# Recurrent heads of a hybrid decoder step: maxima spread by one float32r product, sample outputs in four 32-row groups, prompt states of two heads at once

## The chip, the cores and the metric

The kernel runs on one core of one Trainium2 chip. The metric is the device time of one launch in microseconds (us); less is better. Five engines work side by side: TensorE (PE in the profile; PEld is its weight load), VectorE (DVE), ScalarE (ACT), GpSimd (POOL) and SyncE (SP), which issues most of the transfers.

## The reference, cut to what matters

One inference step of a two-layer trunk over 256 prompt tokens and 8 sample sequences of 8 tokens (320 token columns in all), with a model width of 1024. Layer 0 is half-FFN, mLSTM matrix memory with 8 heads (key width 64, value width 128), half-FFN. Layer 1 is half-FFN, block-sparse attention, half-FFN. The change touches the mLSTM heads alone. For each head, with b the running sum of the log forget gates, li the log input gates, c and n the carried state:

```python
d = jnp.where(causal, b[..., :, None] - b[..., None, :] + li[..., None, :], -jnp.inf)
m_loc = jnp.maximum(b + m, max(d));  w_intra = exp(d - m_loc);  w_inter = exp(b + m - m_loc)
sw = einsum('bhtd,bhsd->bhts', qc, kc) * w_intra
num = w_inter * einsum('bhtd,bhde->bhte', qc, c) + einsum('bhts,bhse->bhte', sw, vc)
den = maximum(abs(w_inter * einsum('bhtd,bhd->bht', qc, n) + sum(sw)), exp(-m_loc));  hc = num / den
c_new = a * c + einsum('bhs,bhsd,bhse->bhde', w, kc, vc)
```

The prompt starts from a zero state, each of the 8 sample sequences from a state of its own. Then hc is normalised per head, multiplied by a sigmoid gate and projected by w_out_a.

## The kernel before, in words

All large products are made in three float32r passes: `passes` (lines 405 to 407) multiplies a high and a low part of the weights with a high and a low part of the activations, 320 columns wide. A chunk is 128 output features over eight 128-row steps, so 24 passes. Weights come by the SP queue into four buffers; ACT (line 844) and DVE (line 1162) split each into `w_hi` and `w_lo`. Every other product is plain float32, which shows in the trace as two passes (two weight loads and two matmuls) for each call; a transpose is one pass.

The stage of the heads runs from the first `head_outputs` to the last. The order on PE is written out by hand. For each head h: `head_outputs(h)`, `head_scores(h + 1)`, `o_chunk(h + 1)` (24 passes of the output-gate projection, which give the other engines time), `head_turn(h)`.

- `head_scores(h)`: line 572 spreads row h of `neg` (minus the running maxima, and the inter-chunk weights, 384 columns) over 128 partitions with an 8-row selector; lines 573 to 575 make the scores of the prompt and the samples from `kT` and `qT`, 64 rows deep.
- DVE `decay(h)` (lines 1368 and 1374) adds columns and masks into `dmat` and makes `qm`, the sample queries spread by sequence; ACT (line 969) takes the exponential; DVE `weights(h)` (line 1383) multiplies scores and weights into `pmat` and raises `p_done`.
- `head_outputs(h)` waits for `p_done`: lines 592 to 594 the prompt outputs, line 596 (64 rows) the samples' own tokens, line 598 four products of `qm` with the loaded states `c0` into the same 64 rows, line 602 the prompt's new state (64 rows of output), line 606 the samples' new states (64 rows deep). It raises `head_o`.
- After `head_o`: DVE `outputs(h)` (lines 1390 to 1399) and ACT `head_squares(h)` (lines 976 and 979) make the variance, POOL (line 1688) the power, ACT `head_scale(h)` (line 988) writes `ot`; `head_turn(h)` transposes `ot` (line 618) and DVE `gated(h)` (line 1415) multiplies with the gate. DVE `states(h)` (line 1407) adds the sample states; POOL sends both states out (lines 1690 and 1692) and loads the next `c0` (line 1694).
- For heads 1 to 6, after `weights(h + 1)`, ACT and DVE also split half a weight unit each (`HALVES`).

DVE works in the order outputs(h), decay(h + 1), states(h), weights(h + 1), half split, keep_gate(h + 1), gated(h), gate_half(h + 1). ACT works in the order head_squares(h), head_scale(h), decay(h + 1), half split, tanh(h + 1).

Earlier, `turn_rows` (line 531) transposes the gate rows into `cols`, once. In the attention of layer 1, outside the change, line 749 and line 758 already write their results in four groups of 32 partitions, one product after the other: these are 128 rows deep, 32 columns of weights, 128 columns moving.

Of the kernel before, what the change touches and what calls it, by code (L numbers as in the profile page):

```python
# [20 lines left out]
TP, NB, TS = 256, 8, 8  # L21
# [5 lines left out]
H = 8  # L27
# [16 lines left out]
R_SEL, R_HALF, R_MUL, R_NEG, R_DEL, R_M0 = 0, 1024, 1280, 1600, 1920, 1928  # L44
R_COLS = 2248
# [22 lines left out]
def trunk_program(nc, w_in, w_out, w_a, w_oa, w_kv, w_q, w_ob, w_gate, x_in, par_in, con_in, row_in,  # L68
# [6 lines left out]
    with ctx:  # L75
# [25 lines left out]
        row = sb("row", [8, R_COLS])  # L101
        par = sb("par", [128, P_COLS])
# [6 lines left out]
        with ExitStack() as ov:  # L109
            with ExitStack() as own:  # L110
# [6 lines left out]
                rows = sb("rows", [128, T], f32, own)  # L117
# [6 lines left out]
                neg = sb("neg", [8, 384], f32, own)  # L124
                mt = sb("mt", [8, T], f32, own)
# [4 lines left out]
                qm = sb("qm", [128, 2, 4 * (NS + 2 * TS)], f32, own)  # L130
                c0 = sb("c0", [128, 2, 4, DV + 1], f32, own)
                cn = sb("cn", [128, 4, DV], f32, own)
                cpn = sb("cpn", [DK, DV], f32, own)
# [26 lines left out]
        sel = row[:, R_SEL:R_SEL + 1024].rearrange("k (h p) -> k h p", h=H)  # L160
# [57 lines left out]
        zero_done = sem("zeros_set")  # L218
        head_s = sem("head_scores_done")
# [100 lines left out]
        def _(sp):  # L320
# [76 lines left out]
            sp.wait_ge(cp_out_s, 16 * H)  # L397
# [4 lines left out]
        def _(pe):  # L402
# [122 lines left out]
            def turn_rows():  # L525
# [3 lines left out]
                for t in range(3):  # L529
                    w = 128 if t < 2 else NS  # L530
                    mm = pe.transpose(bank[6][0:w, t * 128:t * 128 + 128], rows[:, t * 128:t * 128 + w], ident)
# [30 lines left out]
            def head_scores(h):  # L562

                hp, r = h // 2, slice(64 * (h % 2), 64 * (h % 2) + 64)
                if h == 0:
                    pe.wait_ge(pair_free, P_A + 7)
                    pe.wait_ge(tr_free, 8)
                else:
# [3 lines left out]
                pe.matmul(bank[4][:, 0:384], sel[:, h, :], neg[:, :], start=True, stop=True)  # L572
# [5 lines left out]
            def head_outputs(h):  # L578
# [85 lines left out]
            pe.wait_ge(cp_done, H)  # L664
# [164 lines left out]
        def _(sc):  # L829
# [80 lines left out]
            def first_post():  # L910
                split_at(1)
                root_of(0)

# [30 lines left out]
            sc.activation(rows[64:72, :], fa[:, :], ACT.Exp).then_inc(rows_b, 1)  # L944
            sc.activation(neg[:, T:384], fa[:, TP:T], ACT.Exp).then_inc(rows_b, 1)
            sc.wait_ge(mt_done, 1)
            sc.activation(rows[96:104, :], mt[:, :], ACT.Exp, scale=-1.0).then_inc(rows_b, 1)
            sc.wait_ge(aw_done, 2)
            sc.activation(rows[32:40, :], g40[0:8, :], ACT.Exp).then_inc(rows_b, 1)
# [10 lines left out]
            sc.activation(cols[0:NS, 2, :], bank[6][0:NS, 256:384], ACT.Copy).then_inc(cols_done, 1)  # L960
# [10 lines left out]
            def head_squares(h):  # L971

                sc.wait_ge(head_o, h + 1)
                if h >= 1:
                    sc.wait_ge(cp_out_s, 16 * h)
                sc.activation(cpn[:, :], bank[2][0:DK, 0:DV], ACT.Copy).then_inc(cp_done, 1)
# [53 lines left out]
            def after_oa():  # L1030
# [8 lines left out]
                sc.wait_ge(cp_out_s, 16 * H)  # L1039
# [109 lines left out]
        def _(ve):  # L1149
# [178 lines left out]
            ve.tensor_copy(rows[0:8, :], tmp[:, :]).then_inc(rows_a, 1)  # L1328
# [7 lines left out]
            ve.wait_ge(rows_b, 2)  # L1336
# [26 lines left out]
            def decay(h):  # L1363
# [9 lines left out]
                for half in range(2):  # L1373
                    ve.tensor_tensor(
                        qm[64 * half:64 * half + 64, h % 2, :].rearrange("p (a x) -> p a x", a=4)[
# [455 lines left out]
```

## Time and profile before

| | |
|---|---|
| Median of 3 runs (lowest, highest) | 1300.69 us (1300.65, 1302.66) |
| The profiled execution's own time | 1301.33 us |
| Its span, first to last instruction | 1299.5 us |
| PE busy | 1265.3 us (97%) |
| DVE / ACT / POOL busy | 735.6 / 582.1 / 102.8 us |
| Mean granted clock of TensorE | 0.995 of full speed |
| HBM traffic | 154 GB/s over the span |

The profiled execution stands 0.64 us above the median of the runs, and 1.83 us of its own time lie outside its span. Matmuls overlap in the record: each shows some 0.16 us of latency after its columns, so the cost of one is read from the distance between starts, not from its duration. The stage of the heads lies from about 318 to 392 us.

### The profile page before, as it was taken

What the parts mean: (1) busy time and instruction counts of PE and PEld (TensorE: products, weight loads), DVE (VectorE), ACT (ScalarE), POOL (GpSimd) and SP (SyncE); (2) the same over time, 40 slices, a digit from 0 to 9 for tenths busy, and PEclk for the clock granted to TensorE, in tenths of its full rate; (3) what the DMA queues carried; (4) which work ended last, traced back from release to release, by engine and by line L of the source; (5) the groups of instructions that cost most, each with busy time, mean ns of one, the idle gap of its engine ahead of it and who ended that gap; (6) DMA issues with size and microseconds to landing.
All of it is one profiled execution on the core that took longest, in us unless ns stands there. A gap on an engine that the chain in (4) does not pass through costs nothing.

```text
span 1299.5 us, 21993 instructions
## 1 busy us (share of the span) xinstructions
PE 1265.3 (97%) x8841; PEld 1232.9 (95%) x8841; DVE 735.6 (57%) x1151; ACT 582.1 (45%) x922; POOL 102.8 (8%) x118
## 2 busy tenths in 40 slices
PE   6999999999999999999999999999998999999996
PEld 6999999999888999999999999999996899999996
DVE  7556554564666665554454555654555565655443
ACT  6445443453334555534343554533344364544332
POOL 2000000101333000000000000000020020000011
PEclk9999999999999999999999999999999999999998
DMA  8444344543224434434553644334458834343441
GB/s 297 162 140 151 121 134 148 196 133 127 89 92 140 151 138 161 142 99 156 168 180 135 220 156 157 134 110 148 163 179 299 329 123 163 137 161 108 133 147 40
DMA packets 36121, 200.52 MB, mean 154 GB/s; under 512 B 4426, under 2 KB 6602, under 8 KB 20570
## 3 DMA queue, kind: packets, MB, share of 16 engines
q1 hardware_dynamic: 33858, 192.37, 42.6%
q0 software_dynamic: 2208, 7.39, 1.7%
q8 instruction: 37, 0.61, 0.2%
q14 instruction: 18, 0.15, 0.0%
HBM read 193.17 MB, written 6.57 MB: 154 GB/s over the span
## 4 chain that ended last, share of the span: by engine, by line
PE 93%; DMA 2%; DVE 1%; issue 1%; ACT 1%; SPq 1%; POOL 0%; POOLq 0%; DVEq 0%; ACTq 0%
PE bank L405 29%; PE bank L407 29%; PE bank L406 29%; DMA raw<-vc_in 1%; PE bank L606 1%; PE bank L598 1%; DVE h_lo L1174 1%; PE bank L572 1%; DMA raw<-kc_in 0%; DMA raw<-w_in 0%; PE bank L573 0%; PE bank L521 0%; SPq L381 0%; PE bank L510 0%; ACT h_hi L865 0%
## 5 line engine op out<-in xcount | busy, mean ns | idle before, releaser
L405 PE MATMUL bank<-h_hi,w_hi 128*128 128x320 f32 x1920 | 598.0, 311 | 15.8 <-DVE h_lo L1174 14.2
L407 PE MATMUL bank<-h_hi,w_lo 128*128 128x320 f32 x1920 | 594.5, 310 | 0.0
L406 PE MATMUL bank<-h_lo,w_hi 128*128 128x320 f32 x1920 | 594.5, 310 | 0.0
L844 ACT ACTIVATE w_hi<-raw 128x1024 fp32r<-128x1024 f32 (+1 forms) x368 | 336.0, 960 | 461.0 <-PE bank L407 456.4
L1162 DVE TENSOR_TENSOR w_lo<-raw,w_hi 128x1024 fp32r<-128x1024 f32 (+1 forms) x368 | 393.1, 1109 | 116.4 <-ACT w_hi L844 116.1
L405 PEld LDWEIGHTS bank<-h_hi,w_hi 128*128 128x128 f32 x1920 | 361.7, 188 | 19.7 <-DVE w_lo L1162 12.0
L406 PEld LDWEIGHTS bank<-h_lo,w_hi 128*128 128x128 f32 x1920 | 361.7, 188 | 0.2
L407 PEld LDWEIGHTS bank<-h_hi,w_lo 128*128 128x128 f32 x1920 | 361.5, 188 | 0.0
L406 PE MATMUL bank<-f_lo,w_hi 128*128 128x320 f32 x704 | 217.5, 309 | 0.0
L407 PE MATMUL bank<-f_hi,w_lo 128*128 128x320 f32 x704 | 217.5, 309 | 0.0
L405 PE MATMUL bank<-f_hi,w_hi 128*128 128x320 f32 x704 | 217.4, 309 | 0.0
L405 PEld LDWEIGHTS bank<-f_hi,w_hi 128*128 128x128 f32 x704 | 132.2, 188 | 0.0
L407 PEld LDWEIGHTS bank<-f_hi,w_lo 128*128 128x128 f32 x704 | 132.2, 188 | 0.0
L406 PEld LDWEIGHTS bank<-f_lo,w_hi 128*128 128x128 f32 x704 | 132.2, 188 | 0.0
L1188 DVE TENSOR_TENSOR work<-bank,rms 128x320 f32<-128x320 f32 x88 | 43.2, 491 | 151.3 <-PE bank L407 150.8
L883 ACT ACTIVATE f_hi<-work 128x320 f32 (+1 forms) x88 | 41.6, 472 | 123.0 <-DVE work L1196 123.0
L1203 DVE TENSOR_TENSOR f_lo<-work,f_hi 128x320 f32 (+1 forms) x88 | 43.3, 492 | 66.2 <-ACT f_hi L883 66.2
L1652 POOL TENSOR_TENSOR sqsum<-sqsum,sq 128x320 f32<-128x320 f32 x49 | 52.1, 1064 | 276.6 <-ACT sq L862 274.5
L1649 POOL COPY sqsum<-sq 128x320 f32<-128x320 f32 x7 | 6.6, 942 | 724.0 <-ACT sq L862 723.9
L1208 DVE SCALAR_TENSOR_TENSOR x<-bank,x 128x320 f32<-128x320 f32 x32 | 15.7, 492 | 74.1 <-PE bank L407 74.1
L1174 DVE SCALAR_TENSOR_TENSOR h_lo<-x,par,h_hi 128x320 fp32r<-128x320 f32 x56 | 47.9, 892 | 13.0 <-ACT h_hi L865 13.0
L1196 DVE TENSOR_TENSOR work<-work 128x320 f32<-128x320 f32 x88 | 42.7, 486 | 6.6 <-ACT work L879 6.6
(195 smaller groups left out, 652.8 us busy)
## 6 DMA issues: line engine op xcount, KB each, us to landing
raw<-w_in SPq DMA_DIRECT2D x88, 1024.0 KB, 4.8
raw<-w_out SPq DMA_DIRECT2D x64, 704.0 KB, 4.1
raw<-w_a SPq DMA_DIRECT2D x12, 1024.0 KB, 4.8
raw<-w_kv SPq DMA_DIRECT2D x8, 1024.0 KB, 4.8
raw<-kc_in SPq DMA_DIRECT2D x16, 512.0 KB, 4.5
raw<-vc_in SPq DMA_DIRECT2D x16, 512.0 KB, 7.0
raw<-w_oa SPq DMA_DIRECT2D x4, 1024.0 KB, 5.9
raw<-w_q SPq DMA_DIRECT2D x4, 1024.0 KB, 4.8
```

The costliest lines, as they stand in the source:

```text
L405: pe.matmul(out, wh, mh, start=first, stop=False)
L406: pe.matmul(out, wh, ml, start=False, stop=False)
L407: return pe.matmul(out, wl, mh, start=False, stop=last)
L844: sc.activation(w_hi[:, n_at % 2, part * w:part * w + w], raw[:, raw_of(n_at) % RAW, part * w:part * w + w], ACT.Copy).then_inc(hi_done, 1)
L883: sc.activation(dst, up[:, k_at % 2, :], ACT.Copy).then_inc(hid_hi, 1)
L1162: ins = ve.tensor_tensor(w_lo[:, n_at % 2, c], raw[:, raw_of(n_at) % RAW, c], w_hi[:, n_at % 2, c].bitcast(f32), ALU.subtract)
L1174: ve.scalar_tensor_tensor(out=h_lo[:, m, :], in0=x[:, m, :], scalar=par[:, P_G + KT * norm + m:P_G + KT * norm + m + 1], in1=h_hi[:, m, :] ...
L1188: ve.tensor_tensor(gate[:, k_at % 2, :], bank[b][:, 0:T], rms[:, :], ALU.mult).then_inc(gate_ready, 1)
L1196: ve.tensor_tensor(up[:, k_at % 2, :], up[:, k_at % 2, :], act[:, k_at % 2, :], ALU.mult).then_inc(hid_ready, 1)
L1203: ve.tensor_tensor(lo, up[:, k_at % 2, :], hi.bitcast(f32), ALU.subtract).then_inc(hid_lo, 1)
L1208: ve.scalar_tensor_tensor(out=x[:, m, :], in0=bank[4 + m % 2][:, 0:T], scalar=0.5, in1=x[:, m, :], op0=ALU.mult, op1=ALU.add).then_inc(x_r ...
L1652: gp.tensor_tensor(sqsum[:, :], sqsum[:, :], sq[:, m % 2, :], ALU.add).then_inc(sum_done, 1)
```

## The change

- The selector is no longer loaded with the constants. It is a tile of its own, `sel`, 40 rows deep, in float32r, made by POOL (zeros) and ACT (two copies of the identity, into rows 0 to 7 and 32 to 39) in the first FFN. `neg` is split into a rounded high part (ACT, rows 0 to 7 of `neg_hl`) and the rest (DVE, rows 32 to 39), and line 572's product becomes one float32r pass over 40 rows.
- Sample outputs are written by pairs of sequences, 16 tokens in each group of 32 partitions. Line 598's four products go first, each into its own group, then four products of `pmat` with `v_tok` in place of line 596's one, all 128 rows deep. `rows` gets 16 more columns, `cols` for the samples' `exp(-m)` is filled by four small products in `turn_rows`, and the third item of `head_turn` is a float32 product with a picked identity (64 columns) instead of a transpose.
- Line 602's prompt state is made for heads h and h + 1 together when h is even (the second into partitions 64 to 127), copied and stored once.

```diff
@@ turn_rows
+                for a in range(4):
+                    at = TP + 2 * TS * a
+                    mm = pe.matmul(bank[6][SLOT * a:SLOT * a + SLOT, 384:392], rows[:, at:at + SLOT],
+                                   ident[:, 96:104], start=True, stop=True, skip_group_check=True)
@@ head_scores
+                    pe.wait_ge(sel_done, 2)
+                    pe.wait_ge(neg_hi, 1)
+                    pe.wait_ge(neg_lo, 1)
...
-                pe.matmul(bank[4][:, 0:384], sel[:, h, :], neg[:, :], start=True, stop=True)
+                pe.matmul(bank[4][:, 0:384], sel[:, h, :], neg_hl[:, :], start=True, stop=True)
@@ head_outputs
-                    pe.wait_ge(cp_done, h)
+                    pe.wait_ge(cp_done, (h + 1) // 2)
...
-                pe.matmul(o[:, 2 * W:3 * W], pmat[0:64, 384:512], v_tok[0:64, 2, h, :], start=True, stop=True)
                 for a in range(4):
-                    pe.matmul(o[0:64, 2 * W:3 * W], qm[:, h % 2, a * NS:a * NS + NS], c0[:, h % 2, a, :],
-                              start=False, stop=(a == 3), skip_group_check=True)
-
-                for t in range(2):
-                    pe.matmul(bank[2][0:64, 0:DV], kw[:, t, h * 64:h * 64 + 64], v_tok[:, t, h, 0:DV],
-                              start=(t == 0), stop=(t == 1))
+                    pe.matmul(o[SLOT * a:SLOT * a + SLOT, 2 * W:3 * W], qm[:, h % 2, a, :], c0[:, h % 2, a, :],
+                              start=True, stop=False, skip_group_check=True)
+                for a in range(4):
+                    at = 384 + 2 * TS * a
+                    pe.matmul(o[SLOT * a:SLOT * a + SLOT, 2 * W:3 * W], pmat[:, at:at + SLOT], v_tok[:, 2, h, :],
+                              start=False, stop=True, skip_group_check=True)
+
+                if h % 2 == 0:
+                    for t in range(2):
+                        for g in range(2):
+                            pe.matmul(bank[2][64 * g:64 * g + 64, 0:DV], kw[:, t, (h + g) * 64:(h + g) * 64 + 64],
+                                      v_tok[:, t, h + g, 0:DV], start=(t == 0), stop=(t == 1),
+                                      skip_group_check=True)
@@ head_turn
-                for t in range(3):
-                    w = 128 if t < 2 else NS
-                    mm = pe.transpose(bank[3][:, t * 128:t * 128 + w], ot[0:w, t, :], ident[0:w, 0:w])
-                mm.then_inc(ot_tr, 1)
+                for t in range(2):
+                    pe.transpose(bank[3][:, t * 128:t * 128 + 128], ot[:, t, :], ident)
+                pe.matmul(bank[3][:, TP:T], ot[:, 2, :], spread_ident, start=True, stop=True).then_inc(ot_tr, 1)
@@ scalar: first_post, gates, head_squares
+                sc.wait_ge(s_con, 48)
+                sc.wait_ge(sel_set, 1)
+                for i in range(2):
+                    sc.activation(sel[32 * i:32 * i + 8, :, :],
+                                  ident[0:8, 0:8].unsqueeze(2).to_broadcast([8, H, 128]), ACT.Copy).then_inc(sel_done, 1)
...
+            sc.wait_ge(rows_b, 2)
+            sc.activation(neg_hl[0:8, :], neg[:, :], ACT.Copy).then_inc(neg_hi, 1)
...
-            sc.activation(cols[0:NS, 2, :], bank[6][0:NS, 256:384], ACT.Copy).then_inc(cols_done, 1)
+            sc.activation(cols[0:NS, 2, 0:96], bank[6][0:NS, 256:352], ACT.Copy)
+            sc.activation(cols[:, 2, 96:104], bank[6][:, 384:392], ACT.Copy).then_inc(cols_done, 1)
...
-                sc.activation(cpn[:, :], bank[2][0:DK, 0:DV], ACT.Copy).then_inc(cp_done, 1)
+                if h % 2 == 0:
+                    if h >= 2:
+                        sc.wait_ge(cp_out_s, 16 * (h // 2))
+                    sc.activation(cpn[:, :], bank[2][:, 0:DV], ACT.Copy).then_inc(cp_done, 1)
@@ vector
-            ve.wait_ge(rows_b, 2)
+            ve.wait_ge(neg_hi, 1)
+            ve.tensor_tensor(neg_hl[32:40, :], neg[:, :], neg_hl[0:8, :].bitcast(f32), ALU.subtract).then_inc(neg_lo, 1)
@@ gpsimd
+            gp.memset(sel[:, :, :].bitcast(f32), 0.0).then_inc(sel_set, 1)
...
+            gp.memset(neg_hl[:, :].bitcast(f32), 0.0)
+            gp.memset(rows[:, T:T + 2 * TS], 1.0)
...
-                gp.wait_ge(cp_done, h + 1)
-                gp.dma_start(cp_out[h], cpn[:, :]).then_inc(cp_out_s, 16)
+                if h % 2 == 0:
+                    gp.wait_ge(cp_done, h // 2 + 1)
+                    gp.dma_start(cp_out[h:h + 2].rearrange("h d v -> (h d) v"), cpn[:, :]).then_inc(cp_out_s, 16)
```

## Rows read from the trace of the kernel before

**Rows 1.** The page: busy time of the engines, and the chain that ended last.

```profile
PE 1265.3 (97%) x8841; PEld 1232.9 (95%) x8841; DVE 735.6 (57%) x1151; ACT 582.1 (45%) x922; POOL 102.8 (8%) x118
...
PE 93%; DMA 2%; DVE 1%; issue 1%; ACT 1%; SPq 1%; POOL 0%; POOLq 0%; DVEq 0%; ACTq 0%
```

**Rows 2.** Timeline of PE over one head: start, length, line, count, all in us.

```profile
327.33 0.58 PE L618 MATMUL bank<-con,ot 128*128 128x128 f32 x3
327.84 0.49 PE L592 MATMUL bank<-v_tok,pmat 128*128 128x129 f32 x2
328.17 0.39 PE L593 MATMUL bank<-v_tok,pmat 128*128 128x129 f32 x2
328.39 0.39 PE L594 MATMUL bank<-v_tok,pmat 128*128 128x129 f32 x2
328.71 0.49 PE L596 MATMUL bank<-v_tok,pmat 64*128 64x129 f32 x2
329.12 1.10 PE L598 MATMUL bank<-c,qm 128*64 128x129 f32 x8
330.06 0.60 PE L602 MATMUL bank<-v_tok,kw 128*64 128x128 f32 x4
330.59 1.16 PE L606 MATMUL bank<-v_tok,kwm 64*128 64x128 f32 x8
331.68 0.91 PE L572 MATMUL bank<-neg,row 8*128 8x384 f32 x2
332.51 0.70 PE L573 MATMUL bank<-qT,kT 64*128 64x256 f32 x2
333.05 0.38 PE L574 MATMUL bank<-qT,kT 64*128 64x128 f32 x2
333.27 0.33 PE L575 MATMUL bank<-qT,kT 64*128 64x64 f32 x2
333.53 0.41 PE L405 MATMUL bank<-h_hi,w_hi 128*128 128x320 f32 x1
...
337.16 0.58 PE L618 MATMUL bank<-con,ot 128*128 128x128 f32 x3
```

**Rows 3.** Line 596 alone: durations in ns, least, median, greatest.

```profile
L596 PE MATMUL bank<-v_tok,pmat x16: 272/323/374, 318.9 to 389.4; 64*128 64x129 f32 x16
```

**Rows 4.** Timeline of PE in the attention: products in four 32-column groups.

```profile
1011.53 0.65 PE L749 MATMUL bank<-v_tok,p_new 128*32 128x128 f32 x16
1012.19 1.08 PE L758 MATMUL bank<-raw,p_spread 128*32 128x128 f32 x32
```

**Rows 5.** Timeline from head_o to p_done of the next head.

```profile
341.61 0.16 DVE L1390 TENSOR_SCALAR den<-bank 128x3 f32<-128x3 f32 x1 [2.46 <-PE bank L606]
...
342.99 0.16 DVE L1399 SCALAR_TENSOR_TENSOR var<-ssqh,den 128x3 f32<-128x3 f32 x1 [0.64 <-ACT junk L979]
343.47 0.93 DVE L1368 SCALAR_TENSOR_TENSOR dmat<-bank,cols,con 128x256 f32<-128x256 f32 x3 [0.31 <-PE bank L575]
...
344.92 0.59 ACT L969 ACTIVATE dmat<-dmat 128x448 f32<-128x448 f32 x1
...
345.92 0.62 DVE L1383 TENSOR_TENSOR pmat<-bank,dmat 128x448 f32<-128x448 f32 x1
...
347.50 0.49 PE L592 MATMUL bank<-v_tok,pmat 128*128 128x129 f32 x2
```

**Rows 6.** Stretches: length, busy time of PE, PEld, DVE, ACT, POOL, granted clock, DMA share, GB/s.

```profile
318.00:392.00 74.00, 74.00 (x471) 63.44 (x470) 43.14 (x135) 27.00 (x91) 24.97 (x33) 0.98 0.31 104
373.00:376.00 3.00, 3.00 (x12) 3.00 (x13) 2.85 (x11) 2.29 (x5) 1.55 (x3) 0.50 0.07 25
...
1000.00:1024.00 24.00, 20.42 (x349) 14.99 (x349) 14.30 (x47) 11.17 (x38) 0.00 (x0) 1.00 1.03 411
```

**Rows 7.** Timelines of ACT in the gates and in the first FFN.

```profile
287.34 2.01 ACT L844 ACTIVATE w_hi<-raw 128x1024 fp32r<-128x1024 f32 x2 [4.66 <-PE bank L407]
...
35.06 2.01 ACT L844 ACTIVATE w_hi<-raw 128x1024 fp32r<-128x1024 f32 x2 [2.25 <-PE bank L407]
```

More of the change, by code:

```diff
@@ L42 @@
 QB, SLOT, RB = 4, 32, 160
-R_SEL, R_HALF, R_MUL, R_NEG, R_DEL, R_M0 = 0, 1024, 1280, 1600, 1920, 1928
-R_COLS = 2248
+R_HALF, R_MUL, R_NEG, R_DEL, R_M0 = 0, 256, 576, 896, 904
+R_COLS = 1224
 P_G, P_HEAD, P_BI, P_BF = 0, 64, 72, 73
@@ L101, in trunk_program @@
         row = sb("row", [8, R_COLS])
+        sel = sb("sel", [40, H, 128], f32r)
         par = sb("par", [128, P_COLS])
@@ L116, in trunk_program @@
                 kwm = sb("kwm", [NS, 2, NB, DK], f32, own)
-                rows = sb("rows", [128, T], f32, own)
+                rows = sb("rows", [128, T + 2 * TS], f32, own)
                 cols = sb("cols", [128, 3, 128], f32, own)
@@ L124, in trunk_program @@
                 neg = sb("neg", [8, 384], f32, own)
+                neg_hl = sb("neg_hl", [40, 384], f32r, own)
                 mt = sb("mt", [8, T], f32, own)
@@ L129, in trunk_program @@
                 pmat = sb("pmat", [128, 512], f32, own)
-                qm = sb("qm", [128, 2, 4 * (NS + 2 * TS)], f32, own)
+                qm = sb("qm", [128, 2, 4, SLOT], f32, own)
                 c0 = sb("c0", [128, 2, 4, DV + 1], f32, own)
                 cn = sb("cn", [128, 4, DV], f32, own)
-                cpn = sb("cpn", [DK, DV], f32, own)
+                cpn = sb("cpn", [2 * DK, DV], f32, own)
                 ot = sb("ot", [128, 3, DV], f32, own)
@@ L159, in trunk_program @@
         ident, ones = con[:, C_ID:C_ID + 128], con[:, C_ONE:C_ONE + 128]
-        sel = row[:, R_SEL:R_SEL + 1024].rearrange("k (h p) -> k h p", h=H)
+        spread_ident = ident.rearrange("p (a x) -> p a x", a=4)[:, :, 0:2 * TS]
         bank = [ctx.enter_context(nc.psum_tensor(f"bank{i}", [128, 512], f32)) for i in range(8)]
@@ L218, in trunk_program @@
         zero_done = sem("zeros_set")
+        sel_set = sem("selector_zeros_set")
+        sel_done = sem("selector_made")
+        neg_hi = sem("neg_hi_done")
+        neg_lo = sem("neg_lo_done")
         head_s = sem("head_scores_done")
@@ L530, in turn_rows @@
                     w = 128 if t < 2 else NS
-                    mm = pe.transpose(bank[6][0:w, t * 128:t * 128 + 128], rows[:, t * 128:t * 128 + w], ident)
+                    pe.transpose(bank[6][0:w, t * 128:t * 128 + 128], rows[:, t * 128:t * 128 + w], ident)
+                for a in range(4):
+                    at = TP + 2 * TS * a
+                    mm = pe.matmul(bank[6][SLOT * a:SLOT * a + SLOT, 384:392], rows[:, at:at + SLOT],
+                                   ident[:, 96:104], start=True, stop=True, skip_group_check=True)
                 mm.then_inc(rows_t, 1)
@@ L943, in _ @@
             sc.wait_ge(dm_done, 1)
-            sc.activation(rows[64:72, :], fa[:, :], ACT.Exp).then_inc(rows_b, 1)
+            sc.activation(rows[64:72, 0:T], fa[:, :], ACT.Exp).then_inc(rows_b, 1)
             sc.activation(neg[:, T:384], fa[:, TP:T], ACT.Exp).then_inc(rows_b, 1)
             sc.wait_ge(mt_done, 1)
-            sc.activation(rows[96:104, :], mt[:, :], ACT.Exp, scale=-1.0).then_inc(rows_b, 1)
+            sc.activation(rows[96:104, 0:T], mt[:, :], ACT.Exp, scale=-1.0).then_inc(rows_b, 1)
             sc.wait_ge(aw_done, 2)
-            sc.activation(rows[32:40, :], g40[0:8, :], ACT.Exp).then_inc(rows_b, 1)
+            sc.activation(rows[32:40, 0:T], g40[0:8, :], ACT.Exp).then_inc(rows_b, 1)
+            sc.wait_ge(rows_b, 2)
+            sc.activation(neg_hl[0:8, :], neg[:, :], ACT.Copy).then_inc(neg_hi, 1)
             split_at(U_A + 5)
@@ L1327, in _ @@
             ve.wait_ge(zero_done, 4)
-            ve.tensor_copy(rows[0:8, :], tmp[:, :]).then_inc(rows_a, 1)
+            ve.tensor_copy(rows[0:8, 0:T], tmp[:, :]).then_inc(rows_a, 1)
             ve.wait_ge(mt_done, 1)
@@ L1374, in decay @@
                     ve.tensor_tensor(
-                        qm[64 * half:64 * half + 64, h % 2, :].rearrange("p (a x) -> p a x", a=4)[
-                            :, :, 8 * half:8 * half + 8],
+                        qm[64 * half:64 * half + 64, h % 2, :, 8 * half:8 * half + 8],
                         qT[r, hp, TP:T].rearrange("p (a s t) -> p a s t", a=4, s=2)[:, :, half, :],
@@ L1662, in _ @@
             gp.wait_ge(unit_done, U_A)
-            gp.memset(rows[:, :], 0.0).then_inc(zero_done, 1)
+            gp.memset(neg_hl[:, :].bitcast(f32), 0.0)
+            gp.memset(rows[:, T:T + 2 * TS], 1.0)
+            gp.memset(rows[:, 0:T], 0.0).then_inc(zero_done, 1)
             gp.memset(kT[:, :, T:384], 0.0).then_inc(zero_done, 1)
@@ L1734, in _constants @@
     row = np.zeros((8, R_COLS), np.float32)
-    row[:, R_SEL:R_SEL + 1024] = np.repeat(np.eye(8), 128, axis=1)
     row[:, R_HALF:R_HALF + 64] = 1.0
```

12 lines of the change are left out of this document (5 added, 7 removed).

## The prediction, made before the changed kernel ran

> **What bounds the kernel now.** I read the page first: PE is busy 97% of the span, no other engine more than 57%, and 93% of the chain that ended last is PE [rows 1]. Then the stretch of the heads: PE is busy for all of its 74.00 us, though only 43.14 us of DVE and 27.00 us of ACT lie in it [rows 6]. So a microsecond taken from PE here is a microsecond off the end, until something that PE waits for becomes late. The timeline of one head says how PE spends its time; starts are compared, because durations overlap [rows 2]. One head takes 337.16 - 327.33 = 9.83 us, of which the 24 passes of `o_chunk` are 3.63 (333.53 to 337.16). The other 6.20 are small float32 products.
>
> Two prices come out of these rows. First, a float32 pass of 128 columns costs 0.11 us, however few rows or weight columns it uses: L593 to L594 is 0.22 for two. Second, a change of shape of the array costs extra: L594 to L596 (128 rows deep to 64) is 0.32 where two passes are 0.22, so PE stands 0.10 before the new shape's first load. That load is then not hidden, and the first matmul is another 0.10 longer (374 against 272 ns) [rows 3]. I call these the drain (0.10) and the bare load (0.10 for 128 weight columns; 0.05 for 64 and 0.03 for 32, taken in proportion to columns). A head pays them at the third transpose, L592, L596, L598, L606, L572, L573 and at the chunk: eight times.
>
> **Spread of the maxima.** Before, L572 takes 0.83: two passes of 384 columns at 0.32 are 0.64, the rest is its bare load and the drain behind it. With the drain behind L606 and the bare load at L573, L606 to L574 is 333.05 - 330.59 = 2.46. After, it is one float32r pass. The float32r chunk needs 3.63/24 = 0.15 for 320 columns [rows 2], so 384 columns need 0.17 to 0.18; I take 0.17. The trace shows no product 40 rows deep. I take it as 64 deep, the shape of L606 before it and L573 behind it, so that both changes go: L606 0.97 + 0.17 + L573 0.44 = 1.58, a gain of 0.88 a head. If 40 rows were a shape of their own, both changes would stay (+0.40 a head). Head 0 comes from transposes 128 rows deep and keeps one change: 0.66. Sum: 7 x 0.88 + 0.66 = 6.8 us.
>
> **Sample outputs.** Before: L596 0.41 and L598 0.94, ten passes. After: sixteen passes, 32 weight columns each, in four groups. At 0.11 each they would cost 1.76, a loss. But the attention does just this: 32 passes of L758 have the last start at 1012.19 + 1.08 - 0.27 = 1013.00, so 0.81/31 = 0.026 us a pass, a quarter of 0.11; L749's sixteen have (0.65 - 0.27)/15 = 0.025 [rows 4]. The four groups work at once. So the sixteen cost 0.43, plus bare load 0.03 and drain 0.10: 0.56. (The 0.28 between the end of L749's starts and L758 is a wait for a transfer, no price of the form.)
>
> The Trainium skill puts such packing lower: in "TensorE: Matmul & The Clock Gate", section "Measured speedup vs the span model", four row tiles gave 3.07 times, not four. By that the sixteen would cost 1.76/3.07 = 0.57 instead of 0.43, an estimate that takes 8 x 0.14 = 1.1 us off the gain. The rows here show the full four, and the sum goes by them.
>
> **Prompt state.** Before: L602 to L606 is 0.53 in every head. After: nothing in odd heads; in even heads eight passes with 64 weight columns in two groups. No row shows two groups. Bounds: 0.05 a pass if they overlap as the four do, 0.11 if not. I take 0.05, as the nearest rows overlap fully: 0.43 + bare load 0.05 + drain 0.10 = 0.58. If not, +0.43 in four heads.
>
> Both together: 0.41 + 0.94 + 0.53 = 1.88 becomes 0.56 (odd) or 1.14 (even), a gain of 4 x 1.32 + 4 x 0.74 = 8.2 us.
>
> **Turn.** Before, L618 to L592 is 0.51, and L592 itself is 0.33 instead of 0.22 for its bare load. After, all three items are 128 rows deep: two transposes at 0.11 and two passes of 64 columns. Those still load 128 weight columns each; L575 with 64 moving columns needs 0.26 for two with its drain, so 0.11 each is the upper bound, 0.05 the lower; I take 0.11. That is 0.43 + 0.22 against 0.84: 0.19 a head. The last turn has another change of shape behind it: 0.1. Sum 7 x 0.19 + 0.1 = 1.4 us.
>
> **Added on PE, once.** `turn_rows` gets eight passes of 8 columns in the 32-column shape: 8 x 0.026 + 0.13 for the shape, +0.35 us.
>
> **Added elsewhere, costed at nothing.** ACT's two selector copies (about 1 us each, as half of an L844 group) stand between the first square root and the split of unit 2. PE needs that split only after unit 1; ACT later waits 2.25 us for PE at 35.06, so the delay is used up there [rows 7]. The conversion of `neg` (near 0.5 us on ACT, the same on DVE) delays the split of the next unit by so much; ACT then waits 4.66 us for PE before 287.34 [rows 7]. DVE's new wait for it has the split of the same unit behind it, which waits for ACT anyway. If that cover were gone each would cost its own length, 2 and 0.5 us. POOL's memsets come where it waits for squares. The stores of the prompt state become four of double size on a queue that is idle for most of the stage (24.97 of 74 us busy [rows 6]); the copy on ACT falls away in odd heads, where it overlapped DVE's first steps.
>
> **What is late next.** Behind `head_outputs(h + 1)` stands the chain from `head_o` to `p_done`: 341.61 to 345.92 + 0.62 = 346.54, that is 4.93 us, while PE came to L592 at 347.50, 5.89 after `head_o` [rows 5]. PE's part shrinks by 0.88 + 0.08 to 4.93. The chain shrinks too: `decay` waited 0.31 for L575 and can start behind L1399 at 343.17; the exponential (344.92 to 345.51) still stands behind `head_scale` on ACT, but `states` ends 0.3 earlier, and `pmat` is ready 4.63 after `head_o`. With 0.06 for the semaphore and 0.10 for the load it stands 0.1 ahead of PE. So PE stays the bound, just. If the chain does not move forward, PE waits some 0.2 in each of seven heads: 1.4 us. DVE itself is busy for 43.14 us in the stage [rows 6], over seven and a half heads 5.8 a head, against a new period of 7.44 (9.83 - 0.88 - 0.19 - 1.32, odd) and 8.02 (even).
>
> **Sum.** 6.8 + 8.2 + 1.4 - 0.35 = 16.1 us. The profiled execution takes 1301.33 (span 1299.5 and 1.83 around it) and would take 1285.2. Its time is 0.64 above the median of the runs, so against the median: 1300.69 - 16.1 = 1284.6, the forecast. Nothing behind the heads has a fixed date: weight loads are released by splits of the units before, so they move with PE.
>
> **Rivals.**
> - *The chain or the 40 rows.* If 40 rows are a shape of their own, the gain is 7 x 0.40 smaller, 13.3 us: 1287.4. If `p_done` is late by 0.2 in seven heads, 1286.0. For it: the 0.1 us of slack. Against it: half of L572's cost is changes of shape, and L606 and L573 share one.
> - *Two groups don't overlap.* 1.7 us less: 1286.3. Against: rows 4.
> - *No overlap at all in the heads*, for instance because two products in a row accumulate into the same group. Then 8 x (1.76 - 0.43) = 10.6 and 1.7 go: a gain of 3.8, 1296.9. Against: in L758 they do too, and overlap.
> - *The clock gets better.* In the stretch 373 to 376 the granted clock was 0.50, that is 1.2 GHz, directly after a run of half-filled small products ending in the 8-row spread; everywhere else in the stage it was at 2.4 GHz (mean 0.98) [rows 6]. Three microseconds at half speed cost 1.5 us of PE work (74 x 0.02 by the mean). The change shortens such runs from 6.2 to about 4 us. If the fall goes away where the median run had one, the time is 1283.1.
> - *Slower: the clock gets worse.* Groups of 32 columns with short passes could be taken for idleness, and PE be granted 1.2 GHz in the stage. Every microsecond of PE work at that level costs one more, so the change would lose from 16.1 us of work done at half speed, of a stage of about 58; all of it would give 1284.6 + 58 = 1343. Against: the attention's stretch 1000 to 1024, with passes of this form and even with idle time, has 1.00 [rows 6]. For: the one fall above. The Trainium skill, in "TensorE: Matmul & The Clock Gate", section "Part 1: The HAM clock gate", has activity release the throttle; the trace agrees in that the only fall in the stage came behind its thinnest work.
>
> **How the numbers follow.** Chances: forecast, with small errors of its own and the clock's 1.5 us, 0.70 (own range 1282.8 to 1286.0); chain, 40 rows or two groups 0.21; no overlap 0.04; clock worse 0.03; something unseen of no effect 0.02. The range 1282.5 to 1287.8 leaves out the last three and the far ends. A difference of 0.2% (2.6 us) is about what a measurement can tell from no change. Faster 0.95, same 0.02, slower 0.03.
>
> **What would show it.** Per head, start to start: L606 to the 256-column score product falls from 1.92 to about 1.14; the sixteen sample passes start 0.027 apart; the third item of the turn is followed by L592 without a gap; the period alternates between about 7.4 and 8.0. PE idle before the first output product would show the chain. A 40-row product that starts 0.1 after its neighbour's end, or passes 0.11 apart in the 64-column groups, would show those steps wrong; a granted clock of 0.50 in more than a few microseconds would overturn the whole.

## The result, and the profile after

The changed kernel takes 1284.14 us (median of 4 runs, 1283.85 to 1284.91) against 1300.67 (4 runs, 1300.49 to 1302.66): ratio 0.9867, 95% interval 0.9855 to 0.9878. The forecast was 1284.6. The profiled execution took 1283.96 us with a span of 1282.2. So both the direction and the size came out; the size did so in part by errors of opposite sign, which the experiments separate.

The page of the changed kernel, busy time and the chain that ended last, against [rows 1]:

```profile
PE 1248.3 (97%) x8897; PEld 1222.4 (95%) x8897; DVE 739.0 (58%) x1152; ACT 583.0 (45%) x922; POOL 102.0 (8%) x117
...
PE 91%; ACT 2%; issue 2%; DMA 2%; DVE 1%; SPq 1%; POOL 0%; POOLq 0%; DVEq 0%; ACTq 0%
```

PE lost 17 us of busy time and is still busy 97% of the span, though it now runs 56 more passes. Between 318 and 372 us DVE is busy for 42.39 of 54 us; before, it was 43.14 of 74 [rows 6].

PE's timeline over one head, with the scores of an even head (against [rows 2]). Line 606 is L592 of before, 612 and 616 are L598 and L596, 622 is L602, 627 is L606, 586 to 589 are L572 to L575, 638 and 639 the turn:

```profile
324.93 0.38 PE L638 MATMUL bank<-con,ot 128*128 128x128 f32 x2
325.15 0.33 PE L639 MATMUL bank<-con,ot 128*128 128x64 f32 x2
325.43 0.49 PE L606 MATMUL bank<-v_tok,pmat 128*128 128x129 f32 x2
325.75 0.39 PE L607 MATMUL bank<-v_tok,pmat 128*128 128x129 f32 x2
325.97 0.39 PE L608 MATMUL bank<-v_tok,pmat 128*128 128x129 f32 x2
326.29 0.43 PE L612 MATMUL bank<-c,qm 128*32 128x129 f32 x8
326.54 0.40 PE L616 MATMUL bank<-v_tok,pmat 128*32 128x129 f32 x8
326.87 1.16 PE L627 MATMUL bank<-v_tok,kwm 64*128 64x128 f32 x8
327.78 0.42 PE L586 MATMUL bank<-neg_hl,sel 40*128 40x384 f32 x1
328.04 0.59 PE L587 MATMUL bank<-qT,kT 64*128 64x256 f32 x2
328.48 0.38 PE L588 MATMUL bank<-qT,kT 64*128 64x128 f32 x2
```

The sixteen sample passes take 326.87 - 326.29 = 0.58 us. From the sample-state product to the 128-column score product is 328.48 - 326.87 = 1.61, where it was 2.46. And the same stretch where an even head's outputs are followed by an odd head's scores:

```profile
319.04 0.66 PE L622 MATMUL bank<-v_tok,kw 128*64 128x128 f32 x8
...
320.29 0.48 PE L587 MATMUL bank<-qT,kT 64*128 64x256 f32 x1
320.40 0.38 PE L627 MATMUL bank<-v_tok,kwm 64*128 64x128 f32 x2
320.54 0.42 PE L586 MATMUL bank<-neg_hl,sel 40*128 40x384 f32 x1
320.61 0.38 PE L587 MATMUL bank<-qT,kT 64*128 64x256 f32 x1
320.83 0.38 PE L588 MATMUL bank<-qT,kT 64*128 64x128 f32 x2
```

The prompt states start at 319.04 and the sample states at 319.62, 0.58 later. The first pass of the score product (L587) starts at 320.29, before the last two passes of the product ahead of it, and before the spread (L586). An odd head's `kT` and `qT` lie in rows 64 to 127 of the array, the sample-state product and the spread in rows 0 to 63. The stretch takes 320.83 - 319.62 = 1.21. The prediction had not priced that.

The first output products start at 317.70, 325.43, 332.97, 340.74, 348.28, 356.70, 364.23 and 372.65. Six periods of before were 9.72 to 9.83 and one 11.35, the one with the clock's fall. The periods are now 7.73, 7.54, 7.77, 7.54, 8.42, 7.53, 8.42. Two stand out. Rows of PE, DVE and POOL around the first of them:

```profile
348.33 2.60 DVE L1191 TENSOR_TENSOR w_lo<-raw,w_hi 128x1024 fp32r<-128x1024 f32 x1 [0.32 <-ACT w_hi L864]
348.78 1.05 POOL L1710 TENSOR_TENSOR kwm<-kw,con 64x512 f32<-64x512 f32 x1
...
352.11 0.15 DVE L1419 TENSOR_SCALAR den<-bank 128x3 f32<-128x3 f32 x1
...
356.70 0.49 PE L606 MATMUL bank<-v_tok,pmat 128*128 128x129 f32 x2 [0.52 <-DVE pmat L1412]
```

DVE's half split needs 2.60 us instead of 1.22, starts the denominators late without having idled before them, and PE waits 0.52 for `pmat`. The same happens before 372.65 (0.51). The chain from `head_o` to `p_done` (against [rows 5]) in an ordinary head:

```profile
320.82 0.16 DVE L1419 TENSOR_SCALAR den<-bank 128x3 f32<-128x3 f32 x1 [1.56 <-PE bank L627]
...
322.28 0.93 DVE L1398 SCALAR_TENSOR_TENSOR dmat<-bank,cols,con 128x256 f32<-128x256 f32 x3
...
324.75 0.62 DVE L1412 TENSOR_TENSOR pmat<-bank,dmat 128x448 f32<-128x448 f32 x1
```

It is 325.37 - 320.82 = 4.55 us long (forecast 4.63). PE's first output product starts 0.06 after it and takes 0.32 to the next, the bare load included, though its shape is that of the product ahead. So `p_done` is what releases it, by 0.1 us. This holds for the first output products of heads 1, 3, 5 and 7, which come behind a stretch with the overlap. Heads 2, 4 and 6 do not wait: there `pmat` is ready 0.28 us before L606 starts (in head 4 at 348.00 for 348.28, where in head 1 it was 325.37 for 325.43), L606 follows L639 after 0.17 and takes 0.28 to L607.

The clock (against [rows 6]): between 318 and 372 us it is never below full, in this profile and in that of the repeat (after_again). Behind the length come the busy times of PE, PEld, DVE, ACT and POOL, the granted clock (1.00), the DMA share and GB/s:

```profile
318.00:372.00 54.00, 53.48 (x486) 49.22 (x485) 42.39 (x130) 24.63 (x87) 23.32 (x29) 1.00 0.36 123
```

### The profile page after: what moved, and what is told of

Same layout as the page of the kernel before. It is cut to its first block, busy times and chain, and to the rows that moved or that the text cites. A ratio compares the mean times of both kernels' runs of the same rounds, so it can differ in the third digit from the quotient of the medians.

```text
span 1282.2 us, 22107 instructions
## 1 busy us (share of the span) xinstructions
PE 1248.3 (97%) x8897; PEld 1222.4 (95%) x8897; DVE 739.0 (58%) x1152; ACT 583.0 (45%) x922; POOL 102.0 (8%) x117
## 4 chain that ended last, share of the span: by engine, by line
PE 91%; ACT 2%; issue 2%; DMA 2%; DVE 1%; SPq 1%; POOL 0%; POOLq 0%; DVEq 0%; ACTq 0%
PE bank L412 30%; PE bank L414 29%; PE bank L413 29%; DMA raw<-vc_in 1%; ACT w_hi L864 1%; SPq L388 1%; SPq L389 0%; DMA raw<-w_in 0%; ACT junk L1008 0%; POOL scl L1720 0%; PE bank L528 0%; PE bank L469 0%; PE bank L517 0%; ACT ot L1017 0%; DVE x L1663 0%
```

## The experiments

Theory: PE work went as priced, by passes, groups and changes of shape. On top, product pairs in different row halves overlap (not priced), the clock no longer falls because the 8-row float32 product is gone, and a part is given back because `p_done` becomes the bound and DVE's split meets POOL. Rivals: the gain is mostly clock; shape does not matter; two groups do not overlap; DVE's round alone makes the waits. Each kernel ran with repeats of the kernel before on the same chip: medians 1302.35 (17 runs, 1298.87 to 1303.77) for the first four, 1302.12 (7 runs) for the next four, 1302.71 (14 runs) for the last three.

**One part alone.** Three kernels made from the one before.

*spread_only*: the 40-row float32r product and what feeds it (the edit shown is the product alone).

```diff
-                pe.matmul(bank[4][:, 0:384], sel[:, h, :], neg[:, :], start=True, stop=True)
+                pe.matmul(bank[4][:, 0:384], sel[:, h, :], neg_hl[:, :], start=True, stop=True)
```

> The kernel before with the float32r spread of the maxima alone. Both theories have PE as the bound, with about 1 us of cover in each head (p_done 4.93 us and the first output product 5.89 us after head_o in the trace of before), so nothing is lost to a wait. Theory A, only the pass count and the shape changes count: 6.8 us off, 1293.9. Theory B, the trace of the changed kernel also shows something not priced: for odd heads the 40-row spread (rows 0 to 63 of the array) and the score product (rows 64 to 127) run at the same time, start to start of the sample-state product and the 128-column score product 1.21 us there against 1.61 in even heads, so 4 x 0.4 more: 8.4 us off, 1292.3. If the clock's fall to 1.2 GHz in the stage of the heads came from the 8-row product, it does not appear in this run's profile.

Measured 1291.26 (5 runs, 1290.62 to 1291.76), ratio 0.992 (0.9907 to 0.9933). The periods were 8.46 to 8.56 before odd scores and 8.97 to 9.00 before even ones: 0.85 and 1.3 less than 9.83. That is theory B. No fall of the clock in the stage. Against the median of before it is 11.1 us, more than either theory. Lowest run against lowest run, 1298.87 - 1290.62, both with a mean granted clock of 0.997, it is 8.25, which is theory B. The difference is the clock, below. This profile also shows something that matters later: DVE's half split takes 2.54 to 2.70 us in four heads, and PE waits in none, because it comes to its outputs later than `pmat`. One of them:

```profile
343.22 2.70 DVE L1177 TENSOR_TENSOR w_lo<-raw,w_hi 128x1024 fp32r<-128x1024 f32 x1 [0.32 <-ACT w_hi L852]
```

*samples_only*: the four groups, the turn and `turn_rows`.

```diff
-                pe.matmul(o[:, 2 * W:3 * W], pmat[0:64, 384:512], v_tok[0:64, 2, h, :], start=True, stop=True)
                 for a in range(4):
-                    pe.matmul(o[0:64, 2 * W:3 * W], qm[:, h % 2, a * NS:a * NS + NS], c0[:, h % 2, a, :], ...)
+                    pe.matmul(o[SLOT * a:SLOT * a + SLOT, 2 * W:3 * W], qm[:, h % 2, a, :], c0[:, h % 2, a, :], ...)
+                for a in range(4):
+                    at = 384 + 2 * TS * a
+                    pe.matmul(o[SLOT * a:SLOT * a + SLOT, 2 * W:3 * W], pmat[:, at:at + SLOT], v_tok[:, 2, h, :], ...)
...
```

> The kernel before with the sample outputs in four groups and the new third item of the turn alone; the maxima are spread as before and each head makes its own prompt state. By the prices of the prediction: L596 to L606 was 1.88 us a head and becomes 0.56 + 0.22 x 2 + 0.05 + 0.10 = 1.15, 0.73 off in eight heads, plus 1.4 for the turn, less 0.35: 6.9 us off, 1293.8. Rival, the four groups gain from each other only when the spread's long drain is gone: less than 5 us off. If the clock's fall comes from the 8-row product, it may appear here too.

Measured 1297.23 (6 runs, 1295.46 to 1298.48), ratio 0.9965 (0.9953 to 0.9977). The periods without a fall of the clock are 8.87 to 8.93, so 0.9 a head less, as 0.73 and 0.19 give (0.92). Three of its seven are 10.44 to 10.47: three falls in this profile, two more than in that of before. The time therefore misses the expectation by 3 us while the price is right.

*states_only*: one product for two heads.

```diff
-                for t in range(2):
-                    pe.matmul(bank[2][0:64, 0:DV], kw[:, t, h * 64:h * 64 + 64], v_tok[:, t, h, 0:DV],
+                if h % 2 == 0:
+                    for t in range(2):
+                        for g in range(2):
+                            pe.matmul(bank[2][64 * g:64 * g + 64, 0:DV], kw[:, t, (h + g) * 64:(h + g) * 64 + 64],
...
```

> The kernel before with the prompt states of two heads at once alone. Theory, two 64-column groups overlap fully (eight passes 0.05 us apart): an even head costs as much as before, an odd head loses 0.43 us of passes, 4 x 0.43 = 1.7 us off, 1299.0. Rival, two groups do not overlap: eight passes at 0.11 in even heads, none in odd ones, the same work as before, 0.0 us off.

Measured 1299.56 (12 runs, 1297.35 to 1302.13), ratio 0.9981 (0.9972 to 0.999). Heads with the double product keep their 9.82, heads without take 9.38 or 9.39, 0.44 less; two periods of 11.36 hold a fall. So two groups overlap fully. Of the time, the medians give 2.8 and the lowest runs (1298.87 and 1297.35) 1.5; it could not tell 1.7 from 0.0 as well as the periods do.

Together the parts give 11.1 + 5.1 + 2.8 = 19.0 us against 1302.35, the whole change 1302.12 - 1284.3 = 17.8. These medians hold different numbers of falls of the clock. The seven periods without them (a fall taken as 1.53) are cleaner: 7.6 + 6.2 + 1.3 = 15.1 us for the parts, 13.7 for the whole, so 1.4 us is lost when they come together.

**The clock.** *spread_undone*: the changed kernel with the old spread and what feeds it (again the product alone is shown).

```diff
-                pe.matmul(bank[4][:, 0:384], sel[:, h, :], neg_hl[:, :], start=True, stop=True)
+                pe.matmul(bank[4][:, 0:384], sel[:, h, :], neg[:, :], start=True, stop=True)
```

> The changed kernel with the spread of the maxima as before (8 rows, float32, two passes), sample outputs and prompt states as changed. In the profiles so far the granted clock fell to 1.2 GHz inside the stage of the heads in the three kernels with this product (once, three times and twice, some 1.6 us each) and in none of the six with the float32r product. Theory, the two-pass product causes the falls: at least one in the profile, runs scattered over several us. PE work alone: periods 9.83 - 0.19 - 1.32 = 8.32 and 8.90, so 1290.3 without a fall, and 1292 to 1295 with one to three. Rival, the falls come from the whole length of the small products, which is here shorter by 1.2 us a head than before: no fall, 1290.3 and runs within 1 us.

Measured 1296.35 (9 runs, 1290.84 to 1301.44), ratio 0.9953 (0.9934 to 0.9972). The profile, which took 1296.86, has four falls in the stage; two stretches of it, and the rows of PE ahead of the first (line 577 is the spread):

```profile
332.00:335.00 3.00, 3.00 (x14) 3.00 (x13) 2.79 (x11) 2.29 (x5) 1.03 (x3) 0.51 0.00 0
370.00:373.00 3.00, 3.00 (x13) 3.00 (x12) 2.79 (x9) 2.24 (x5) 1.11 (x2) 0.50 0.03 5
```

```profile
329.61 0.91 PE L577 MATMUL bank<-neg,row 8*128 8x384 f32 x2
...
331.20 0.33 PE L580 MATMUL bank<-qT,kT 64*128 64x64 f32 x2
...
332.20 0.47 PE L407 MATMUL bank<-h_lo,w_hi 128*128 128x320 f32 x1
332.46 0.47 PE L408 MATMUL bank<-h_hi,w_lo 128*128 128x320 f32 x1
```

Full passes of the chunk become longer, 0.47 for 0.31, less than a microsecond after the small products end. A fall costs 1.5 us: the periods with one are 1.52 to 1.55 longer than their like without, here and in before, samples_only and states_only. Four of them off 1296.86 leave 1290.8, beside 1290.3 worked out for no fall and 1290.84 in the lowest run. Where a fall lies is known for the profiled runs alone, but every run of the experiments has its mean granted clock on record, and in spread_undone the time goes with it:

| Time, us | 1290.84 | 1292.1 | 1293.13 | 1295.35 | 1296.35, 1296.86, 1296.96 | 1301.11, 1301.44 |
|---|---|---|---|---|---|---|
| Mean granted clock | 0.997 | 0.996 | 0.995 | 0.993 | 0.992 | 0.988 |

From end to end that is 0.009 of some 1290 us, 11.6 us of clock, for 10.6 us of time: by this estimate none to seven falls. The 38 repeats of the kernel before behave alike: 0.997 in the three runs from 1298.87 to 1300.01, 0.996 or 0.995 from 1300.32 to 1301.2, 0.994 or 0.993 from 1301.91 up.

*spread_8_rows_float32r* leaves the low parts out of the spread:

```diff
-                pe.matmul(bank[4][:, 0:384], sel[:, h, :], neg_hl[:, :], start=True, stop=True)
+                pe.matmul(bank[4][:, 0:384], sel[0:8, h, :], neg_hl[0:8, :], start=True, stop=True)
```

> The changed kernel with a float32r spread of the high parts alone, 8 rows deep; the low parts of the maxima and of the inter-chunk weights are left out of the spread. Theory, price by shape: 8 rows are a shape of their own, so that a change of shape stands before and behind the product and the odd heads lose their overlap, as with 128 rows: 2.5 us slower than the changed kernel, 1286.8, though the product reads five times fewer rows. On the clock: if a thin product lowers the clock by its few rows alone, a fall appears in the stage; if it takes the long two passes, none does and the runs stay within 1.2 us of each other. Rival on time, rows are cheap and 8 cost no more than 40: 1284.1.

Measured 1286.85 (4 runs, 1286.38 to 1287.08), ratio 0.9886 (0.987 to 0.99), no fall in the stage. So a thin product alone does not lower the clock. What brings the falls, absent without it and back with it, is the float32 product over 8 rows, 0.83 us in two passes, among the half-filled products around it; whether by its length, its two passes or its format these runs do not separate.

Counting all thirteen profiles: one, three, two and four falls in the four kernels with the float32 product over 8 rows, none in the stage in the nine without it. Their runs differ in the same way: 2.2 to 10.6 us between lowest and highest with it, at most 1.8 without.

**Price of a shape.** *spread_128_rows*: `sel` and `neg_hl` 128 rows deep, the rest zeros.

```diff
-        sel = sb("sel", [40, H, 128], f32r)
+        sel = sb("sel", [128, H, 128], f32r)
-                neg_hl = sb("neg_hl", [40, 384], f32r, own)
+                neg_hl = sb("neg_hl", [128, 384], f32r, own)
```

> The changed kernel with the spread product 128 rows deep (the rows beyond the 40 are zeros), nothing else. The passes and their length are the same, 0.17 us. Theory, the price is in the changes of shape of the array and in the overlap of the two row halves: each spread gets a change of shape before and behind it (about 0.40 us a head, 7 heads, in head 0 none) and the odd heads lose their overlap (0.4 us in four heads), of which the waits for p_done of the changed kernel (1.0 us in two heads, and small ones) take back about 1.5: 2.5 to 4.5 us slower than the changed kernel, 1286.6 to 1288.6. Rival, depth does not matter and only the number of passes does: 1284.1.

Measured 1286.79 (4 runs, 1286.4 to 1287.06), ratio 0.9884 (0.987 to 0.9899), 2.5 us above the changed kernel. The same columns, yet from the sample-state product to L588 it is 2.00 us in place of 1.61 (even) and 1.21 (odd):

```profile
327.22 1.16 PE L627 MATMUL bank<-v_tok,kwm 64*128 64x128 f32 x8
328.31 0.44 PE L586 MATMUL bank<-neg_hl,sel 128*128 128x384 f32 x1
328.68 0.70 PE L587 MATMUL bank<-qT,kT 64*128 64x256 f32 x2
329.22 0.38 PE L588 MATMUL bank<-qT,kT 64*128 64x128 f32 x2
```

0.39 is the two changes of shape (priced 0.40) and 0.40 the overlap. Eight rows give the same stretch, 1.99, and the same time, 1286.85: it is the depth's shape that costs, not the number of rows, and 40 rows share the shape of 64. Its periods, 8.42 to 8.48 and 7.88, have no wait for `pmat`, so the 2.5 us are what remains of 4 x 0.79 + 3 x 0.39 = 4.3 after the waits of the changed kernel are taken back (some 1.8). Two half splits of 2.60 us are there too, in both kernels, without a wait of PE: a long split costs nothing as long as `pmat` is ready before PE comes.

**The waits.** *keys_early*:

```diff
                 gp.tensor_tensor(scl[:, :], var[:, :], mhalf[:, :], ALU.pow).then_inc(s_pow, 1)
+                if h + 2 < H:
+                    keys_of(h + 2)
...
                     gp.dma_start(c0[:, h % 2, :, :], c0_in[h + 2]).then_inc(c0_load[h % 2], 16)
-                    keys_of(h + 2)
```

> The changed kernel with one instruction of POOL moved: the spread of the keys for head h + 2 stands right behind the power of head h, ahead of the stores, instead of behind them. In the trace of the changed kernel DVE's half split, which reads two SBUF tensors, takes 2.60 us instead of 1.22 in two heads, where POOL's key product starts 0.45 us behind it, and in the next head PE waits 0.52 us for pmat. Theory, the two compete for SBUF: no half split takes 2.60 any more, PE's two waits (1.0 us) go, 1283.1. Rival, the waits come from the length of DVE's round alone, which the move does not change: 1284.1.

Measured 1282.93 (4 runs, 1282.29 to 1283.14), beside 1284.3 (4 runs, 1283.92 to 1284.47) for the changed kernel on the same chip:

> The changed kernel once more, as the measure for the other runs on this chip: 1284.1 us.

1.4 us off, by moving one POOL instruction. All six half splits take 1.22 or 1.23, POOL's product 1.03 in place of up to 1.66, and both waits of PE are gone:

```profile
345.48 1.03 POOL L1710 TENSOR_TENSOR kwm<-kw,con 64x512 f32<-64x512 f32 x1
...
347.86 1.23 DVE L1191 TENSOR_TENSOR w_lo<-raw,w_hi 128x1024 fp32r<-128x1024 f32 x1 [0.32 <-ACT w_hi L864]
```

Both instructions read two SBUF tensors. Where they overlapped in the changed kernel, one or the other was held up: in two heads DVE (2.60), in the other three POOL (1.60 to 1.66), though DVE had started some 0.5 us earlier each time. What decides between them, and that it is the reading of SBUF that collides, is not shown. *chain_short* is keys_early and takes 0.9 us out of the chain besides; PE's wait for the sample states moves behind the output products with it:

```diff
                     decay(h + 1)
-                    states(h)
                     weights(h + 1)
+                    states(h)
...
-                    head_scale(h)
                     decay(h + 1)
+                    head_scale(h)
...
```

> keys_early, and the chain from head_o to p_done made shorter: ACT takes the exponential ahead of the scaling of the outputs, DVE the weights ahead of the sample states, and PE waits for the sample states only at the product that overwrites their bank. p_done should come about 3.7 us after head_o instead of 4.5. Theory, in the changed kernel p_done is the bound in most heads (the first output product starts without its load hidden, 0.10 us in each, and 0.5 in two): the periods become 7.62 (even) and 7.44 (odd) in place of 7.73 and 7.54 with two of 8.42, 2.1 us off the changed kernel, 1282.0. Rival, DVE's whole round is the bound (7.2 us with a half split): no more than keys_early gives, 1283.1.

Measured 1282.25 (4 runs, 1281.81 to 1282.34). `pmat` is ready 3.65 us after `head_o`. The periods are 7.67 and 7.49, with no bare load behind the turn; the sums of the prediction without the overlap counted 8.02 and 7.44, and with it 7.62 and 7.44. That gives 0.7 us beyond keys_early and 0.25 less than expected: the prices are 0.05 too low a head. DVE's round, which the rival had as the bound, was not.

**Row halves.** *rows_apart*: chain_short, and for even heads the operands of the spread stand once more in rows 64 to 103.

```diff
+                q = slice(64 * (1 - h % 2), 64 * (1 - h % 2) + 40)
-                pe.matmul(bank[4][:, 0:384], sel[:, h, :], neg_hl[:, :], start=True, stop=True)
+                pe.matmul(bank[4][:, 0:384], sel[q, h, :], neg_hl[q, :], start=True, stop=True)
...
-                for i in range(2):
+                for i in range(4):
                     sc.activation(sel[32 * i:32 * i + 8, :, :],
```

> chain_short, and for even heads the spread product uses a second copy of its operands in rows 64 to 103, so that in every head it lies in the other half of the rows from the score products behind it. Theory, products in different row halves run at the same time: the stretch from the sample-state product to the 128-column score product of even heads (2, 4, 6) falls from 1.61 to about 1.2 us, as odd heads show already; as a whole up to 1.2 us less if DVE's round allows it (a period of 7.04 against DVE's 7.2: 3 x 0.25), 1281.2. Rival, the short time of the odd heads comes from something else (kT's rows, or the head order): the stretch stays at 1.6 and the time at that of chain_short.

Measured 1283.82 (4 runs, 1282.8 to 1284.54), slower than chain_short. The even periods did fall, from 7.49 to 7.31 or 7.33, but not by 0.4. And PE waited where nobody had looked, in unit 2 of the first FFN, for the split behind four selector copies instead of two:

```profile
PE bank L412 <- DVE w_lo L1194: 1.7, 1, 1.7
```

This is the cover that the prediction took for the two copies, used up by four: two copies (2.1 us) are hidden, four (4.3 us) cost 1.7 us at the least. *rows_apart_late* makes the other two copies later:

```diff
             split_at(U_A + 3)
+            for i in (2, 3):
+                sc.activation(sel[32 * i:32 * i + 8, :, :],
+                              ident[0:8, 0:8].unsqueeze(2).to_broadcast([8, H, 128]), ACT.Copy).then_inc(sel_done, 1)
             split_at(U_A + 4)
```

> rows_apart with the two extra selector copies of ACT moved out of the first FFN to the gates, where ACT waits 5 us for PE. rows_apart had the heads' periods shorter by 0.18 us in three heads than chain_short but PE waited 1.7 us for the split of unit 2 in the first FFN, which stands behind the four copies. Theory, the copies alone cost this wait: it goes, and the time is that of chain_short less 0.6 us, 1281.7. Rival, the second copy of the operands slows something else: 1282.3 or more.

Measured 1281.62 (5 runs, 1280.88 to 1282.36), ratio 0.9845 (0.9832 to 0.9858), the fastest kernel of the study, 2.7 us below the changed one. The scores of an even head (here 587 is the spread, 629 the sample states, 589 the 128-column score product):

```profile
341.42 0.82 PE L629 MATMUL bank<-v_tok,kwm 64*128 64x128 f32 x5
341.97 0.44 PE L587 MATMUL bank<-neg_hl,sel 40*128 40x384 f32 x1
342.08 0.50 PE L629 MATMUL bank<-v_tok,kwm 64*128 64x128 f32 x3
...
342.85 0.38 PE L589 MATMUL bank<-qT,kT 64*128 64x128 f32 x2
```

The spread, now in rows 64 to 103, starts in the middle of the sample-state product in rows 0 to 63. It saves its own 0.18 us (342.85 - 341.42 = 1.43 for 1.61), not 0.4: the expectation took an odd head's saving for an even one, where only one product can move to the other half instead of four.

## Why the prediction was right, and where it was not

- *PE is the bound, a microsecond less of it is one less at the end.* Held. From the first output product to the first matmul of the output projection it was 394.57 - 318.12 = 76.45 us, now 377.69 - 317.70 = 59.99, of these 16.46 us 1.5 by the fall; the rest of the span moved by under a microsecond. The 256-column score product follows the sample states after 328.04 - 326.87 = 1.17, for 1.14.
- *Four groups at once.* Held: 0.58 against 0.56, and not the rival's 1.76. The estimate by the Trainium skill, "TensorE: Matmul & The Clock Gate", section "Measured speedup vs the span model", had 0.57 for the passes alone, so 0.70 with the change of shape; the measurement decides for the full four. That row of the page is for tiles of rows; the groups here are tiles of columns.
- *Two groups at once.* Open before, now 0.58 as taken, and shown by states_only.
- *40 rows share the shape of 64.* Held, and the price of a change, 0.20, held within 0.01 (spread_128_rows). The spread's saving in even heads was 0.85 for 0.88. In odd heads it was 1.25: **the term that failed is this one, by 0.4 in four heads, 1.6 us too small**, because products in different row halves overlap. The Trainium skill has this: "TensorEngine Tiling (Array Packing)", section "Key Properties", has different tiles load and multiply in parallel. The trace agrees in odd heads, 1.21 for 1.61 us. The prediction used this for columns and not for rows.
- *The turn and `turn_rows`.* Where PE does not wait, the third item takes 0.17 to L606 and L606 takes 0.28, against 0.22 and 0.22: the sum held. `turn_rows` adds 0.18 (the eight passes of 8 columns), not 0.35.
- *PE stays ahead of the chain by 0.1 us.* The chain's length was right (4.55 for 4.63), the conclusion was not, because PE had become 0.4 faster behind the overlapped stretches. There, at the outputs of heads 1, 3, 5 and 7, it lost some 0.15 us: 0.10 of wait and 0.05 of a load that was hidden no longer. Behind the others it kept its cover. That DVE's mean load left room was true too, and did not help: a split met POOL's product and took 1.4 us longer, which cost 0.65 in each of two heads (8.42 against 7.77). Keys_early and chain_short give back 1.4 and 0.7: 2.1 us in all, the price of this step. So the rival that the prediction gave for the chain, 0.2 in each of seven heads, had the wait right, and neither its places nor its size.
- *Clock.* Given as a rival with 1.5 us. It was part of the result. Lowest run against lowest run, 1298.87 (of 42 runs) less 1283.85 (of 8), is 15.0: PE work and waits. (The profiles give 15.4 with the fall taken off: 14.9 from the first output product on, and 0.5 ahead of it, 0.65 by head 0's spread less 0.18 by `turn_rows`.) The other 1.5 of the 16.5 us, and nearly 3 against the repeats of before, are falls of the clock that no longer happen. The slower rival did not come: the stage stayed at 2.4 GHz with the packed groups. But it was the spread that kept it there. With the groups packed and the old spread in place, samples_only had three falls and spread_undone four, and the median runs a mean granted clock of 0.993 and 0.992 beside 0.994 for the repeats of the kernel before; whether the groups make the falls more frequent there is open.
- *Selector copies and the conversion, costed at nothing.* Held for two copies; rows_apart shows how near the edge. (The 24.97 us that the prediction took for the use of a queue are POOL's busy time; nothing hung on it.)

So the sum is 16.1 + 1.6 (row halves) + 1.5 (clock) - 2.1 (waits) - 0.5 (prices some 0.05 too low a head, and 0.2 less than priced in the last head) = 16.6, for 16.5 measured. The range held, but partly by luck of signs. With the waits removed the time leaves it: chain_short takes 1282.25, below the lower end of 1282.5. The closeness of 1284.6 is luck to the same degree.

What stays open: which part of the thin stretch the clock answers to, the length of the 8-row product, its float32 format or its sum with its neighbours (a long product of 40 rows was not tried), whether the packed groups matter to it, and which of DVE and POOL is held up when they meet.

## What to carry to other kernels

Price a small product by shape, group and neighbours, not by its size: a change of row depth cost 0.2 us here, more than the product itself, and products in other rows or columns of the array ran beside each other. When a bound engine gets a fifth faster in a stage, redraw the round of every other engine with its longest instruction, not its mean, and look at what runs at the same time on the engine beside it. And compare the lowest run, not only the median, of a kernel whose runs scatter.

## What the runs showed of the hardware

- A product that starts in the other half of the rows ran before and beside products issued ahead of it: L587 at 320.29 ahead of L586 at 320.54.
- A float32 product over 8 rows, 0.83 us long, went with one to four falls of the granted clock from 2.4 to 1.2 GHz in a stage of 70 to 76 us though PE was busy throughout, each some 1.5 us of time; a float32r product over the same 8 rows, or over 40 or 128, with none.
- Two elementwise instructions of DVE and POOL, each with two SBUF inputs, held each other up: 2.60 for 1.22 us on DVE, or 1.60 to 1.66 for 1.03 on POOL, with DVE the first to start in both cases.
